# The split rows of a mixture-of-experts layer laid out by k instead of by column number

## The reference

```python
g_idx = argmax(t @ w_group)                 # one of 4 groups
top_v, top_i = top_k(e_sel, 2)              # 2 of its 4 experts
for gi in range(4):
    hg = einsum('td,edf->tef', t, w_gate[gi])
    hu = einsum('td,edf->tef', t, w_up[gi])
    act = silu(hg) * hu * gates
    out = out + einsum('tef,efd->td', act, w_down[gi])
```

## Time and profile before

| what | value |
| --- | --- |
| median of 3 runs | 772.08 us |
| span of the profiled execution | 771.4 us (inside the runs' 770.12 to 772.75) |
| TensorE busy | 740.5 us, 96% of the span |
| VectorE busy | 273.6 us |
| ScalarE busy | 140.7 us |
| mean rate of the transfers | 320 GB/s |
| gather products, L861 | 64, 17.2 us of busy time |

### The profile page before, as it was taken

The page is one execution under the profiler, slowest core; times in us unless marked ns, Lnnn a source line. Parts: engine busy times, 40 slices in busy tenths (PEclk is TensorE's granted clock), DMA queues, the critical chain, the costliest instruction groups (busy, mean ns, idle before and its releaser), DMA issues.

```text
span 771.4 us, 8317 instructions
## 1 busy us (share of the span) xinstructions
PE 740.5 (96%) x3174; PEld 347.9 (45%) x3174; DVE 273.6 (35%) x654; ACT 140.7 (18%) x347; POOL 27.1 (4%) x49
## 2 busy tenths in 40 slices
PE   9999999999999999889999999999999999988996
PEld 6345565774333333233445554494333333323444
DVE  1213341354327233223222465253435423332323
ACT  3000231321111111100221143232111111110131
POOL 3300000000000000000000000000000000000000
PEclk9999999899999999999999999989999999999998
DMA  9996241939999999999999690237999999999911
GB/s 345 298 381 263 107 164 69 421 126 406 421 421 421 420 421 421 421 421 420 385 297 288 265 365 1 93 126 297 424 421 421 421 421 420 423 421 421 402 60 55
DMA packets 49224, 246.67 MB, mean 320 GB/s; under 512 B 4552, under 2 KB 5672, under 8 KB 24608
## 3 DMA queue, kind: packets, MB, share of 16 engines
q1 hardware_dynamic: 46816, 240.77, 79.0%
q0 software_dynamic: 2048, 5.07, 1.9%
q10 hardware_dynamic: 320, 0.29, 0.1%
HBM read 245.04 MB, written 2.63 MB: 321 GB/s over the span
## 4 chain that ended last, share of the span: by engine, by line
PE 65%; DMA 18%; SPq 10%; issue 3%; DVE 2%; ACT 1%; POOLq 0%; POOL 0%; DVEq 0%; ACTq 0%
PE bank L619 24%; PE bank L884 16%; SPq L420 10%; PE bank L901 8%; DMA weights<-in_moe_w_down_dram 7%; DMA weights<-in_moe_w_up_dram 7%; DMA weights<-in_even_w_in_dram 4%; PE bank L914 2%; PE bank L861 2%; PE bank L1052 1%; PE bank L605 1%; PE bank L810 1%; PE bank L817 1%; PE bank L893 1%; PE bank L666 1%
## 5 line engine op out<-in xcount | busy, mean ns | idle before, releaser
L884 PE MATMUL bank<-weights,expert_rows 128*64 128x512 f32 x1024 | 228.0, 594 | 14.5 <-DMA weights<-in_moe_w_up_dram 14.5
L619 PE MATMUL bank<-weights,normalised 128*128 128x512 f32 (+1 forms) x512 | 219.3, 582 | 3.2 <-DMA weights<-in_even_w_in_dram 1.7
L884 PEld LDWEIGHTS bank<-weights,expert_rows 128*64 128x64 f32 x1024 | 75.3, 137 | 158.3 <-issue 157.5
L619 PEld LDWEIGHTS bank<-weights,normalised 128*128 128x128 f32 x512 | 95.1, 190 | 109.5 <-issue 107.2
L901 PE MATMUL bank<-weights,hidden_turned 128*64 128x512 f32 x256 | 58.8, 598 | 1.3 <-DVE hidden_turned L1767 0.6
L901 PE MATMUL bank<-weights,hidden_turned_odd 128*64 128x512 f32 x256 | 58.8, 598 | 0.6 <-DMA weights<-in_moe_w_down_dram 0.6
L1351 ACT ACTIVATE gate_tanh<-bank 128x256 f32<-128x256 f32 x32 | 12.4, 386 | 199.5 <-PE bank L884 199.5
L1797 DVE TENSOR_TENSOR gather_onehots<-bank,expert_outputs 128x512 fp32r<-128x512 f32 x32 | 22.1, 692 | 55.5 <-ACT expert_outputs L1221 55.3
L1221 ACT ACTIVATE expert_outputs<-bank 128x512 fp32r<-128x512 f32 x32 | 19.1, 597 | 123.8 <-PE bank L901 123.8
L1767 DVE COPY hidden_turned<-bank 128x256 f32<-128x256 f32 x16 | 6.8, 424 | 84.3 <-PE bank L893 84.3
L1767 DVE COPY hidden_turned_odd<-bank 128x256 f32<-128x256 f32 x16 | 6.8, 425 | 81.9 <-PE bank L893 81.9
(11 more groups left out here) (251 smaller groups left out, 619.0 us busy)
## 6 DMA issues: line engine op xcount, KB each, us to landing
weights<-in_moe_w_gate_dram SPq DMA_DIRECT2D x64, 1024.0 KB, 18.8
weights<-in_moe_w_up_dram SPq DMA_DIRECT2D x64, 1024.0 KB, 20.5
weights<-in_moe_w_down_dram SPq DMA_DIRECT2D x64, 1024.0 KB, 22.9
weights<-in_even_w_in_dram SPq DMA_DIRECT2D x5, 2048.0 KB, 30.2
weights<-in_ple_w_gate_dram SPq DMA_DIRECT2D x4, 2048.0 KB, 30.8
weights<-in_even_w_out_dram SPq DMA_DIRECT2D x2, 2048.0 KB, 19.8
weights<-in_odd_w_qkv_dram SPq DMA_DIRECT2D x2, 2048.0 KB, 19.0
weights<-in_odd_w_out_dram SPq DMA_DIRECT2D x4, 1024.0 KB, 21.9
```

Source lines behind the costliest of these rows:

```text
L619: mm = pe.matmul(B[bank][:, 0:width], XT[:, k, tok(t)], w[:, k, :], start=(k == 0), stop=(k == KD - 1))
L884: mm = pe.matmul(bank[j * BLK:(j + 1) * BLK, :].rearrange("p (m f) -> p m f", m=2), rows[:, k, :], W[:, slots, a:a + FF // 2], start=(k == ...
```

## The change

The split rows change their layout. Before, element m * 8 + k of the row lay at place m * 8 + k. After, it lies at place k * 128 + m, so that the 128 elements of one k are neighbours. Three instructions change their access patterns, and none is added, removed or moved:

```diff
-   mm = pe.matmul(B[k][:, :], HSP[part][:, t, k:D:KD], PH[:, t, :], ...
+   mm = pe.matmul(B[k][:, :], HSP[part][:, t, k * P:(k + 1) * P], PH[:, t, :], ...

-   act.activation(HSP[0][:, t, :], H[:, t, :], ACT.Copy, scale=rstd(kn, t))
+   act.activation(HSP[0][:, t, :].rearrange("p (k m) -> p k m", k=KD),
+                  H[:, t, :].rearrange("p (m k) -> p k m", k=KD), ACT.Copy, scale=rstd(kn, t))

-   cols = lambda ap: ap.rearrange("p (m k) -> p m k", k=KD)[:, :, a:b]
+   part = lambda n: HSP[n][:, t, :].rearrange("p (k m) -> p k m", k=KD)[:, a:b, :]
-   dve.scalar_tensor_tensor(out=cols(HSP[1][:, t, :]), in0=cols(H[:, t, :]), scalar=rstd(kn, t),
-                            in1=cols(HSP[0][:, t, :].bitcast(F32)), ...
+   dve.scalar_tensor_tensor(out=part(1), in0=H[:, t, :].rearrange("p (m k) -> p k m", k=KD)[:, a:b, :],
+                            scalar=rstd(kn, t), in1=part(0).bitcast(F32), ...
```

More of the change, by code:

```diff
@@ L860, in gathered @@
                         for part in range(2):
-                            mm = pe.matmul(B[k][:, :], HSP[part][:, t, k:D:KD], PH[:, t, :], start=(t + part == 0),
+                            mm = pe.matmul(B[k][:, :], HSP[part][:, t, k * P:(k + 1) * P], PH[:, t, :], start=(t + part == 0),
                                            stop=(t + part == TT))
@@ L1309, in experts @@
                     act.wait_ge(sem("rstd_ready"), 2 * kn + t + 1)
-                    act.activation(HSP[0][:, t, :], H[:, t, :], ACT.Copy, scale=rstd(kn, t)).then_inc(sem("hs_high"), 1)
+                    act.activation(HSP[0][:, t, :].rearrange("p (k m) -> p k m", k=KD),
+                                   H[:, t, :].rearrange("p (m k) -> p k m", k=KD), ACT.Copy, scale=rstd(kn, t)).then_inc(sem("hs_high"), 1)
                 act.wait_ge(sem("pT_ready"), l + 1)
@@ L1645, in rows_low @@
                 def rows_low(t, a=0, b=KD):
-                    cols = lambda ap: ap.rearrange("p (m k) -> p m k", k=KD)[:, :, a:b]
+                    part = lambda n: HSP[n][:, t, :].rearrange("p (k m) -> p k m", k=KD)[:, a:b, :]
                     dve.wait_ge(sem("hs_high"), 2 * l + t + 1)
-                    dve.scalar_tensor_tensor(out=cols(HSP[1][:, t, :]), in0=cols(H[:, t, :]), scalar=rstd(kn, t),
-                                             in1=cols(HSP[0][:, t, :].bitcast(F32)), op0=ALU.mult, op1=ALU.subtract)\
+                    dve.scalar_tensor_tensor(out=part(1), in0=H[:, t, :].rearrange("p (m k) -> p k m", k=KD)[:, a:b, :],
+                                             scalar=rstd(kn, t), in1=part(0).bitcast(F32), op0=ALU.mult, op1=ALU.subtract)\
                         .then_inc(sem("hs_low"), 1)
```

## The result

The changed kernel is slower: the ratio to the kernel before is 1.0046, with a 95% interval of 1.0028 to 1.0064. Medians are 775.1 us against 772.2 (22 runs each). That is 3.6 us of loss, 2.2 to 4.9, where the forecast was 0.6 us of gain and the range ended at +1.5. Single executions differ a lot: 770.8 to 780.1 after, 766.9 to 779.1 before. The profiled one spans 772.9 us.

What follows compares the result with a forecast made beforehand. Transfers pace the experts' stage, TensorE and its waits what comes ahead, including the gather. Gather -2.1 us and readers +1.5 us sum to -0.6 us, forecast 771.5 us, range 769.7 to 773.6.

Steps and rivals of the forecast that it cites:

- The loads: Gather's TensorE loads: unbroken reading shortens them from 330 to near 185 ns, judged by the scatter's loads on 64 partitions.
- The period: Gather's time per product: 0.244 to 0.218 us, bounds 0.215 to 0.235; with first loads 1.04 us gained a layer.
- The readers: ScalarE's high and VectorE's low part read the residual in 32-byte steps: 0.86 + 0.64 = 1.5 us lost, between 0 and 1.95.
- Where they land: Place by place, the readers' loss costs 0 except in layer 1's first half of the tokens, where it appears fully.
- The second cover: Second token half, both layers: VectorE's 2.12 us wait for the counts absorbs the remaining 0.6 us; cost 0.
- The full 1.5 us comes out late: Layer 1, first token half: the readers delay additions and transposes by 1.5 us, and with them routing, gather and transfers.
- slower through the clock: Rival, chance 0.07: layer 1's longer wait extends 1.2 GHz into the gather, +1.9 us in all, 774.0.
- the one point at which the low clock reaches the gather: Clock rival's condition: low stretch ends some 4 us later, past 514.08 + 1.5; half the run of 24 then loses 2.5 us.
- The argument against it: Against the clock rival: layer 1's unread products come before the gather and are unchanged in number.
- The sum: Whole kernel: 2.1 us gained in the gather and 1.5 lost by the readers give -0.6 us.

Runs made afterwards that it cites:

- e1: Changed kernel with only the gather's half: unbroken loads, residual and split rows walked without gaps (computes another function); 0.9977 of the kernel before, 1.8 us faster.
- e6: Kernel before, with the high and low parts walking their rows in 32-byte steps in layer 0 alone; 1.0017, 1.3 us slower, not told from nothing.
- e5: Kernel before, with the high and low parts walking their rows in 32-byte steps in layer 1 alone; 1.0063, 4.9 us slower.
- e10: Kernel before plus three unused VectorE operations, 1.8 us together, ahead of layer 1's additions, no strided reads by either engine; 1.0066, 5.1 us slower.
- e13: e10 plus eleven unread products on TensorE in its wait ahead of layer 1's transposes; 1.0000 of the kernel before.
- e2: Kernel before, layout and loads kept, with the high and low parts walking their rows in 32-byte steps in both layers; 1.0075, 5.8 us slower.
- e8: Changed kernel with VectorE's low parts in half rows, moved behind the additions and the routing; 0.9996 of the kernel before, 3.9 us better than the changed kernel.
- e3: Changed kernel, but the high and low parts read the residual without gaps and write in 512-byte steps; 1.0050 of the kernel before.
- e9: e5 plus ten unread products on TensorE in the wait ahead of layer 1's transposes; 1.0039 of the kernel before.

## Why the prediction was wrong

**The loads: right.** 188 ns where 185 was forecast, and the comparison with the scatter's loads, on 64 partitions, held for 128.

**The period: inside its bounds, near the pessimistic side.** In e1, whose clock was full in both gathers, neighbouring products of layer 1 start 0.227 us apart (median; 0.231 in the run of 8) against 0.243 and 0.242 before. That is inside 0.215 to 0.235, but not 0.218. The loads of the run of 24 take 5.33 us there, where 5.2 was forecast. In layer 1 the gain is 0.47 + 0.23 = 0.70 us, not 1.04. Timing gives 1.8 us for both layers (0.2 to 3.3), which doesn't tell 1.4 from 2.1. It fits a gain that passes through the saturated transfers.

**The readers: right in kind, a little small.** ScalarE +1.00 against 0.86, VectorE +0.79 against 0.64: 1.8 us and not 1.5, within the bound of 1.95. ScalarE alone went past a doubling of its pace per element (0.98 ns more on 0.84), which I had taken for its upper end.

**Where they land: right in layer 1, and in layer 0 for the first tokens.** VectorE's idle time there is 0.99 of the old 2.77 us, 1.8 less. The second cover was weaker than argued. I had read 2.12 us of idle time ahead of the counts as cover, but its length depends on the clock of the unread products. In the changed kernel's profile they ran faster, ended early, and TensorE waited 0.84 us. e6 puts the price in layer 0 at -0.6 to 3.2 us, so whether it matters stays open.

**The failed step: "The full 1.5 us comes out late".** The step took a wait of 1.5 us to cost 1.5 us. Layer 1's readers cost 4.9 us (e5), a bare wait of 2 us 5.1 (e10), and the filled one 0.0 (e13). In e5 and e10 an execution has some 7 us more at 1.2 GHz than one of the kernel before, an estimated 2.3 to 2.4 us on top of the wait. What stood in the step's place is the third rival, "slower through the clock", which had a chance of 0.07. It was priced by the one point at which the low clock reaches the gather. That point was not needed: TensorE is on the chain from the transposes until the routing's last part, so a further microsecond at 1.2 GHz costs there as well. The rival was weighed as an all-or-nothing event of one execution, while it is an expectation over executions. The argument against it (the unread products stand before the gather) held in the profiles of e2, e5 and e10, where layer 1's low stretch ends before the gather; it did not touch the price ahead of them. The unequal runs of the kernel before, 770.1 to 772.8 with three of them, had already hinted at something that differs between executions.

**The sum.** With 1.4 for the gather and the measured 5.8 for the readers it is +4.4, against 3.6 (2.2 to 4.9) measured. From path and clock it is an estimated -1.4 + 1.8 + 2.3 = +2.7, also inside the interval. The 2.3 stand for 6.8 us more at 1.2 GHz (mean clock 0.9870 against 0.9914).

**What stays open.** In the traces, e10's layer 1 is about 3 us longer than before from the first transposes to the gather's end: 2.0 of wait and 1 of low clock. That is just inside the 2.9 to 7.2 of its timing; the mean clocks bring the estimate to 4.4. They say how much low clock an execution has, and not where. What sets it in a single execution, besides the idle wait, was not found: e8's profile has 10.3 us of it in layer 1, where its transposes never wait.

## What to carry to other kernels

Moving a stride from one engine to another moves its price, and what counts is who waits at the new place: here the load had been mostly hidden behind products, and the two readers stood bare in a chain. Price a new wait of TensorE by more than its length where its work around it is already thin, look at the granted clock on both sides of it, and test it by filling it. An idle time that ends on TensorE's own filler work is no fixed cover, since the length of that work depends on the clock (3.76 us at 1.2 GHz, 2.03 at 2.4).

## What the runs showed of the hardware

- A step of 32 bytes costs every engine that was tried. TensorE's float32r load of 128 columns took 330 ns with it and 188 without. ScalarE took 1.0 us more for 1024 elements and VectorE 0.8. A pattern of 16 bytes and a gap of 16 had cost VectorE nothing. The Trainium skill, in Advanced Engine Details and Errata, section SBUF Cachelines, has the line of 16 bytes that fits all of these.
- Writing in steps of 512 bytes costs ScalarE nearly the same, 2.07 us against 1.16 (e3).
- Products of 512 columns in float32r, each with an unbroken load, started 0.23 us apart at full clock (e1, medians of 0.227 and 0.231). The chain's 5.78 us for a run of 24 holds its first load and last product too.
- Low clock and time go together: over the 116 executions of the kernel before, whose mean granted clock lay between 0.983 and 0.998, each further microsecond at 1.2 GHz went with 0.34 us.
- The low clock in the same unchanged code differs between executions: layer 0 of e10 was at 1.2 GHz for 10 us, layer 0 of e9 not at all. The first window is e10's, the second e9's.

```profile
152.60:162.60 10.00, 10.00 (x44) 9.58 (x43) 6.38 (x24) 0.11 (x1) 0.00 (x0) 0.50 0.60 249
```

```profile
146.00:162.00 16.00, 15.03 (x100) 12.55 (x99) 9.39 (x34) 3.92 (x8) 1.11 (x2) 1.00 0.97 402
```
